# Modulation of two transformer blocks: weights laid out turned, one fused product and sum by VectorE per 128 outputs, no sums by TensorE or GpSimd

## The reference, cut to what matters

```
# first block: dilated and differential attention, then a gated FFN
mod = silu(c) @ w_ada + b_ada                  # 2048 -> 6 x 2048
sh_a, sc_a, gt_a, sh_f, sc_f, gt_f = split(mod, 6)
h = rmsnorm(x, g_pre_attn) * (1 + sc_a) + sh_a
mix = attention(h @ w_in)                      # w_in: 2048 x 6144
x = x + gt_a * rmsnorm(mix @ w_out, g_post_attn)
h = rmsnorm(x, g_pre_ffn) * (1 + sc_f) + sh_f
f = (silu(h @ w_gate) * (h @ w_up)) @ w_down
x = x + gt_f * rmsnorm(f, g_post_ffn)
# second block: mLSTM and a gated convolution side by side
mod = silu(c_2) @ w_ada_2 + b_ada_2            # 2048 -> 3 x 2048
shift, scale, gate = split(mod, 3)
h = rms_norm(x, norm1_w_2) * (1 + scale) + shift
x = x + gate * (merged(h @ w_in_2 + b_in_2) @ w_out_2)
out = rms_norm(x, normf_w_2)
```

## Time and profile before

| | |
|---|---|
| time, median of 3 runs | 2428.45 us (2428.37 to 2431.06) |
| the profiled execution: its own time | 2428.18 us |
| its span | 2426.4 us |
| PE busy | 2335.1 us, 96% |
| DVE busy | 1910.8 us, 79% |
| ACT busy | 1120.4 us, 46% |
| POOL busy | 94.5 us, 4% |
| chain that ended last | PE 84%, DVE 11%, ACT 2% |

### The profile page before, as it was taken

How to read it: one execution, slowest core, us unless ns; L and a number is a source line. 1 busy time by engine, 2 the same in 40 slices (tenths; PEclk the granted TensorE clock), 3 DMA queues, 4 the chain that set the end, 5 groups by cost and what they waited for, 6 DMA issues and landing times.

```text
span 2426.4 us, 26656 instructions
## 1 busy us (share of the span) xinstructions
PE 2335.1 (96%) x10405; PEld 1923.6 (79%) x10405; DVE 1910.8 (79%) x2446; ACT 1120.4 (46%) x1469; POOL 94.5 (4%) x60
## 2 busy tenths in 40 slices
PE   3789999989999999999989999999999999999998
PEld 3578788878888888788868888888888888888887
DVE  7888898977888988999865567898778697555875
ACT  3344566554444444444464333444445544444453
POOL 0000000000110100113100000000000001000000
PEclk8889999999999999999999999999999999999999
DMA  9978788958778778799845655465666557655553
GB/s 348 360 276 303 275 290 330 355 210 282 277 275 295 280 275 292 268 333 354 320 146 199 219 192 201 169 218 192 205 208 206 204 188 269 209 196 195 191 191 122
DMA packets 89694, 601.64 MB, mean 248 GB/s; under 512 B 11072, under 2 KB 11248, under 8 KB 18784
## 3 DMA queue, kind: packets, MB, share of 16 engines
q1 hardware_dynamic: 85520, 588.94, 68.2%
q0 software_dynamic: 3040, 10.37, 1.4%
q10 hardware_dynamic: 1008, 0.62, 0.1%
HBM read 597.75 MB, written 2.14 MB: 247 GB/s over the span
## 4 chain that ended last, share of the span: by engine, by line
PE 84%; DVE 11%; ACT 2%; issue 2%; DMA 1%; DVEq 0%; ACTq 0%
PE PS L1216 19%; PE PS L1217 19%; PE PS L1225 19%; PE PS L1200 16%; PE PS L1205 8%; DVE BIAS L1635 5%; DVE LO L1617 3%; PE PS L1307 1%; DMA RAW<-in_w_down 1%; ACT HI L691 1%; PE PS L1333 0%; DMA R<-in_k_inv 0%; PE PS L1551 0%; DVE R L1665 0%; DMA RAW<-in_w_first 0%
## 5 line engine op out<-in xcount | busy, mean ns | idle before, releaser
L691 ACT ACTIVATE HI<-RAW 128x1024 fp32r<-128x1024 f32 x808 | 854.5, 1061 | 1192.0 <-PE PS L1225 727.1
L1617 DVE TENSOR_TENSOR LO<-RAW,HI 128x1024 fp32r<-128x1024 f32 x808 | 1018.8, 1265 | 422.0 <-ACT HI L691 418.1
L1216 PE MATMUL PS<-HI,XH 128*128 128x512 f32 x2176 | 868.3, 399 | 7.6 <-DVE XL L1871 3.1
L1217 PE MATMUL PS<-HI,XL 128*128 128x512 f32 x2176 | 854.6, 393 | 0.0
L1225 PE MATMUL PS<-LO,XH 128*128 128x512 f32 x2176 | 587.1, 391 | 2.9 <-DVE LO L1617 2.9
L1216 PEld LDWEIGHTS PS<-HI,XH 128*128 128x128 f32 x2176 | 413.0, 190 | 97.1 <-ACT HI L691 4.7
L1225 PEld LDWEIGHTS PS<-LO,XH 128*128 128x128 f32 x2176 | 410.5, 189 | 91.1 <-DVE LO L1617 4.9
L1217 PEld LDWEIGHTS PS<-HI,XL 128*128 128x128 f32 x2176 | 413.1, 190 | 84.4 <-issue 1.0
L1635 DVE SCALAR_TENSOR_TENSOR BIAS<-RAW,CACT,BIAS 128x1024 f32<-128x1024 f32 x270 | 348.8, 1292 | 8.2 <-DMA RAW<-in_w_mod 0.3
L1200 PE MATMUL PS<-HI,XH 128*128 128x512 f32 x1056 | 326.8, 391 | 3.8 <-issue 2.2
L1200 PE MATMUL PS<-HI,XL 128*128 128x512 f32 x1056 | 325.6, 390 | 0.0
(11 more groups left out here) (256 smaller groups left out, 888.6 us busy)
## 6 DMA issues: line engine op xcount, KB each, us to landing
RAW<-in_w_second SPq DMA_DIRECT2D x208, 1024.0 KB, 4.9
RAW<-in_w_mod SPq DMA_DIRECT2D x144, 1024.0 KB, 5.1
RAW<-in_w_ffn SPq DMA_DIRECT2D x88, 1024.0 KB, 4.9
RAW<-in_w_first SPq DMA_DIRECT2D x64, 1024.0 KB, 5.1
RAW<-in_w_down SPq DMA_DIRECT2D x44, 1024.0 KB, 5.0
BIAS<-in_b_in SPq DMA_DIRECT2D x40, 256.0 KB, 5.1
X<-in_x SPq DMA_DIRECT2D x1, 2048.0 KB, 10.8
R<-mod_rows POOLq DMA_DIRECT2D x4, 512.0 KB, 4.9
```

The costliest lines, as they stand in the source:

```text
L691: act.activation(HI[:, (it["half"] + hf) % HLS, :], RAW[:, it["slot"], hf * 1024:(hf + 1) * 1024], ACT.Copy).then_inc(s.hi_ready, 1)
L1216: pe.matmul(PS[:, bank + u, :], XH[:, 2 * n + kk, rows], hi, start=start and kk == 0, stop=False)
L1217: pe.matmul(PS[:, bank + u, :], XL[:, 2 * n + kk, rows], hi, start=False, stop=False)
L1617: dve.tensor_tensor(LO[:, slot, :], RAW[:, it["slot"], hf * 1024:(hf + 1) * 1024], HI[:, slot, :].bitcast(F32), ALU.subtract).then_inc(s.l ...
```

## The change

The weights of the modulation are laid out the other way round: an A now holds 128 outputs on the partitions and all 2048 inputs along the row. Silu(c) is loaded broadcast to all partitions (`C_ROW`, 1 MB, in the place of the accumulators BIAS; `C_ROW_2` for the second block from chunk 96 on), and one DVE instruction (L1543) multiplies a whole A by it and sums along the row into one column of `MOD`. So every A ends with 128 finished outputs. The accumulator chains, the sums by PE, `reduce_ada` and the additions on POOL, MODT and its turn by PE are gone. Shift and scale of the first modulation are laid out in turn, tile by tile, so that four A make one pair of tiles; `first_scale`, `x_pair` and `x_low` go by pairs, at halves 6q and 6q + 4, and the body puts 4 A, 2 A and 2 A ahead of the three W of each q. The number of chunks of either kind stays. Gates go from MOD to DRAM and back as a broadcast row (`gate_rows`).

```diff
 def first_body():
-    body = [("A",)] * 8
-    for q in range(1, 4):
+    body = []
+    for q in range(4):
         for g in range(EARLY):
-            body += [("A",)] * (1, 3, 4)[g] + [("W", EARLY * (q - 1) + g)]
-    for c in range(9, 64):
+            body += [("A",)] * (4, 2, 2)[g] + [("W", EARLY * q + g)]
+    for c in range(12, 64):
...
+            def gate_rows(n, rows):
+
+                v = mod_dram[:, n * D:(n + 1) * D]
+                pool.wait_ge(s.gate_ready, n + 1)
+                pool.dma_start(v[0].rearrange("(t p) -> p t", p=P), MOD[:, GATE_AT[n]:GATE_AT[n] + NK]).then_inc(s.gate_out, 16)
+                pool.wait_ge(s.gate_out, 16 * n + 16)
+                pool.dma_start(rows, v.to_broadcast([P, D])).then_inc(s.gg_in, 16)
...
+            act.dma_start(C_ROW, c_rows[0:1, :].to_broadcast([P, D])).then_inc(s.c_in, 16)
...
-            act.activation(CACT[:].rearrange("p a k -> p (a k)"), CT, ACT.Silu).then_inc(s.cact_ready, 1)
+            act.activation(C_ROW, C_ROW, ACT.Silu).then_inc(s.cact_ready, 1)
...
             def x_pair(n):
 
-                act.wait_ge(s.mod_ready, n // 2 + 1)
+                act.wait_ge(s.mod_ready, n + 1)
...
-                if h < 8 * EARLY and h % (2 * EARLY) < 2:
-                    x_pair(first_half(h)[1])
+                if h < 8 * EARLY and h % (2 * EARLY) in (0, 4):
+                    x_pair(h // EARLY)
...
+                    if h == 20:
+                        act.wait_ge(s.c_2_in, 16)
+                        act.activation(C_ROW_2, C_ROW_2, ACT.Silu).then_inc(s.cact_ready, 1)
...
-            def ada_sum(a, hf):
-                pe.wait_ge(s.ada_step, a * 16 + 16)
-                bank_7_free()
-                used[0] += 1
-                if hf is None:
-                    for t in range(8):
-                        m = pe.matmul(PS[:, 7, t:t + 1], acc_of(a)[:, t * P:(t + 1) * P], ONES[:, 0:1], start=True, stop=True,
-                                      skip_group_check=True)
-                else:
-                    m = pe.matmul(PS[:, 7, :], ONES[:], acc_of(a)[:, hf * 512:(hf + 1) * 512], start=True, stop=True)
-                m.then_inc(s.ada_sum, 1)
...
             def ada_chunk(sec, it):
-                a = sec.ada_group(0, it["ada"])
-                which, acc = vector_of(a), acc_of(a)
+
+                a = sec.ada_chunk(0, it["ada"])
+                w = RAW[:, it["slot"], :]
                 dve.wait_ge(landed[it["slot"]], sec.landed(0, it))
-                for kk in range(2):
-                    k = 2 * it["step"] + kk
-                    w = RAW[:, it["slot"], kk * 1024:(kk + 1) * 1024]
-                    if k == 0:
-                        if 2 <= a <= ADA_BY_PE:
-                            dve.wait_ge(s.ada_sum, SUMS[a - 2])
-                        if a > ADA_BY_PE:
-                            dve.wait_ge(s.acc_reduced, a - ADA_BY_PE)
-                        dve.tensor_scalar(acc, w, CACT[:, which, 0:1], None, ALU.mult).then_inc(s.ada_step, 1)
-                    else:
-                        dve.wait_ge(s.ada_step, a * 16 + k)
-                        dve.scalar_tensor_tensor(out=acc, in0=w, scalar=CACT[:, which, k:k + 1], in1=acc,
-                                                 op0=ALU.mult, op1=ALU.add).then_inc(s.ada_step, 1)
...
+                if a == ADA_OF_C:
+                    dve.wait_ge(s.cact_ready, 2)
+                dve.tensor_tensor_reduce(w, w, C_ROW if a < ADA_OF_C else C_ROW_2, 1.0, 0.0, ALU.mult, ALU.add,
+                                         MOD[:, a:a + 1]).then_inc(s.ada_step, 1)
...
+            def first_scale(n):
+
+                v = MOD[:, 4 * n:4 * n + 4]
+                dve.wait_ge(s.ada_step, 4 * n + 4)
+                link(dve.tensor_tensor(v, v, BCOL[:, 4 * n:4 * n + 4], ALU.add))
+                dve.scalar_tensor_tensor(out=SCALE[:, 2 * n:2 * n + 2], in0=MOD[:, 4 * n + 1:4 * n + 4:2], scalar=1.0,
+                                         in1=COL[:, 2 * n:2 * n + 2], op0=ALU.add, op1=ALU.mult).then_inc(s.mod_ready, 1)
...
                 if it["kind"] == "A":
                     ada_chunk(sec, it)
-                    if it["j"] == 0:
+                    if it["j"] == 1:
+                        first_rstd()
+                    if it["j"] == 2:
                         angles()
                         first_columns()
-                    if it["j"] == 1:
-                        first_rstd()
-                    if it["j"] == 8:
-                        first_scale(0)
+                    if it["ada"] < ADA_FIRST and it["ada"] % 4 == 3:
+                        first_scale(it["ada"] // 4)
```

More of the change, by code:

```diff
@@ L229, in __init__ @@
         self.n_halves = 2 * sum(kind == "W" for kind, *_ in body)
-        self.n_ada = sum(kind == "A" for kind, *_ in body) // 8
+        self.n_ada = sum(kind == "A" for kind, *_ in body)
         assert self.n_chunks % RAWS == 0 and self.n_halves % HLS == 0
@@ L237, in __init__ @@
             slot_gain[slot] += 16
-            self.items.append(dict(kind=kind, what=what, slot=slot, j=j, half=half, ada=ada // 8, step=ada % 8,
+            self.items.append(dict(kind=kind, what=what, slot=slot, j=j, half=half, ada=ada,
                                    landed=slot_gain[slot]))
@@ L409, in build @@
         JUNK = region(6144, 2048)
-        CT = region(16512, 32)
+        C_ROW_2 = region(13312, 2048)
         ANG = region(16640, NT, 96)
@@ new lines, in ada_chunk, with gate @@
+                dve.tensor_tensor_reduce(w, w, C_ROW if a < ADA_OF_C else C_ROW_2, 1.0, 0.0, ALU.mult, ALU.add,
+                                         MOD[:, a:a + 1]).then_inc(s.ada_step, 1)
+                for n, at in enumerate(GATE_AT):
+                    if a == at + NK - 1:
+                        gate(n)
+                if a == MOD_AT[1] + 31:
+                    modulation(2)
+            def gate(n):
+                v = MOD[:, GATE_AT[n]:GATE_AT[n] + NK]
+                dve.wait_ge(s.ada_step, GATE_AT[n] + NK)
+                add = dve.tensor_tensor(v, v, BCOL[:, GATE_AT[n]:GATE_AT[n] + NK], ALU.add)
+                if n == 2:
+                    add.then_inc(s.gate_ready, 1)
+                    return
+                link(add)
+                dve.tensor_tensor(v, v, COL[:, 114 + 16 * n:130 + 16 * n], ALU.mult).then_inc(s.gate_ready, 1)
@@ L2420, in chunks, with in_turn @@
         return np.stack([np.concatenate(p, axis=2).reshape(P, 2048) for p in pieces])
[L2422 to L2429 removed]
+    turned = [w[name].T.reshape(-1, P, D) for name in ("w_ada", "w_ada_2")]
+    def in_turn(a, b):
+        return np.concatenate([np.stack([a[0:NK], a[NK:2 * NK]], axis=1).reshape(-1, *a.shape[1:]), a[2 * NK:], b])
     def first():
@@ L2450, in columns @@
         return np.concatenate([np.asarray(v).reshape(-1, P).T for v in vectors], axis=1)
-    b_ada = np.asarray(inputs["b_ada"])[0]
-    return {"w_mod": chunks(modulation()), "w_first": chunks(first()), "w_ffn": chunks(ffn()),
+    b_ada, b_ada_2 = (np.asarray(inputs[name])[0].reshape(-1, P) for name in ("b_ada", "b_ada_2"))
+    return {"w_mod": in_turn(*turned), "w_first": chunks(first()), "w_ffn": chunks(ffn()),
             "w_down": w["w_down"].reshape(NKF, P, 2048), "w_second": chunks(second()),
```

237 lines of the change are left out of this document (62 added, 175 removed).

## The result

The changed kernel takes 2434.86 us (median of 11 runs, 2433.88 to 2436.99), the kernel before 2430.84 (median of 11 runs beside it). Two runs of the kernel before, of 2629.38 and 5899.89 us, lie far above the others and are left out of the comparison; without them its median is 2428.91. The ratio of the other runs is 1.0022, 95% interval 1.0013 to 1.0032: the changed kernel is slower by some 5 us, hardly more than a measurement tells from no change. The profiled execution took 2434.49 us, with a span of 2432.7, 6.3 more than in the earlier trace rows.

The account below looks back on a forecast made before the run. PE bounds the kernel (busy 2335.1 of 2426.4 us), paced by DVE in the first 160 us. From 2428.18: + 23.4 start and groups, - 14.3 PE's sums, - 3.0 DVE's relief, - 4.4 POOL, giving 2429.9 us, range 2415 to 2445.

Parts of the forecast that it names:

- The start and the groups: First 160 us: half 1 at 55.3, then 37.3 us per group in place of 31.76 as DVE stands waiting.
- The load of C_ROW ahead of IDENT: Start, ACT's queue: the 1 MB ahead of IDENT adds up to 2.6 us, so the turn starts at 26.1.
- Halves 19 to 23: End of the early part: five halves take 13.6 + 2.8 = 16.4 us, 2.8 being the low clock's price.
- the loss at half 24: End of the early groups: half 24 starts at 183.6 in place of 160.21, a loss of 23.4 us.
- the third rival: Early groups longer than 37.3 us, DVE waiting for an A's load; decides from 1 us per group (2433.4); chance 0.27.
- The half pace: Rival on the new DVE product: an A takes 4.4 us, the kernel 2545 us; chance 0.03.
- The sums and the relief: Behind the start: PE's dropped sums gain 14.3 us (10.5 to 17), DVE's cheaper A 3.0 (0 to 10).
- POOL: Reductions that stretch DVE's LO halves, and the gate's additions, end: a gain of 4.4 us (bounds 3 and 5).
- costed at nothing: Gates' way through DRAM: no cost, covered over 100 us ahead of use; without cover, 0 to some 10 us.
- The most likely case: Whole kernel: losses and gains cancel, 2423.6 to 2433.3 us, within 0.2%; chance 0.44.

Follow-up runs that it names:

- e1: Changed kernel with the old order of the early chunks, both pairs of a group modulated ahead of its first half: 2413.48 us, ratio 0.9936.
- e4: Changed kernel with eight A first, then three W in each early group, both pairs modulated ahead of the first half: 2412.90 us, ratio 0.9937.
- e7: Kernel of e2 with one extra DVE instruction of 0.42 us behind each of the first 32 A: 2442.07 us.
- e11: Changed kernel with IDENT loaded ahead of C_ROW on ACT's queue: 2432.39 us.
- e5: Kernel of e2 with PE's sums put back as products nobody reads: 2443.00 us.
- e6: Kernel of e2 with six of GpSimd's eight partition reductions put back, on numbers nobody reads: 2432.28 us, ratio 1.0008.
- e9: Kernel of e6 with one extra DVE instruction of 0.42 us behind each A from chunk 80 on: 2437.90 us, ratio 1.0029.
- e10: Kernel of e2 with one extra DVE instruction of 0.42 us behind each A from chunk 80 on, without the reductions: 2431.38 us, ratio 1.0003.
- e3: Changed kernel with the edits of e1 and e2 together: 2406.95 us, ratio 0.991.
- e2: Changed kernel with the gate turned on DVE and stored in 64 pieces of 128 bytes, not 2048 of 4 bytes: 2431.61 us, ratio 1.0008.

## Why the prediction held, step by step

**The start and the groups** were right in mechanism. Half 0 was put at 38.2 and came at 39.20, half 1 at 55.3 and 55.58. The group was put at 37.3 and was 36.4, 36.5 and 35.4; the A in it cost 2.21 and not 2.3, since the read of the sum hides, which is 0.7 us per group, and the rest was not traced. Halves 19 to 23: 16.4 predicted, 16.43 measured. So the loss at half 24 was 20.1 where the sum had 23.4. That the order makes most of it is shown by e1 and e4 (half 24 comes 22.6 us earlier), that each us of a group counts over three times by e7. The load of C_ROW ahead of IDENT, which the prediction put at 2.6 us for IDENT, costs 3.3 at half 24 (e11). The mechanism of the third rival, DVE waiting for the load of an A, did not occur: from 40 to 157 us DVE waits for ACT alone.

**The half pace** of the fused product with two operands in SBUF did not occur: 2.285 us for 2048 columns are 896 columns per us, against 1024 / 1.22 = 839 in the earlier trace rows, the row with one tensor read twice. The Trainium skill (page "Vector Engine (DVE) Microarchitecture Reference", section "Points that are easy to get wrong") says that instructions of the form S2S2D2_STT halve their throughput with two sources in SBUF that are not bf16, by which the prediction estimated 4.4. The trace disagrees with that for this instruction, which it calls CUSTOM_DVE_ANT_0; whether the page means it, no run can tell.

**The sums and the relief** were put at 14.3 and 3.0 and came to 17.7 together; e5 gives the sums 13.5 by places and 11.4 by medians. The bounds of the sums were added up wrongly: with all column sums at 3.4 they make 17.5 and not 17, with all at 1.94 11.7 and not 10.5. The forecast doesn't hang on that.

**POOL** was put at 4.4 and the stretch of trace shows 4.9, but the reason given, the stretched LO halves, does not carry it, and that this number came out is luck. The earlier trace rows was misread: its last row holds three reductions (at 996.83, 1066.76 and 1133.41) and not six, the rest of POOL's 37.35 us being mostly the gate's additions, and the row of 174.08 us, which served as the measure without them, holds two. e6 shows that reductions alone cost little, e9 and e10 that they cost more with a dearer A; what the 4.9 us were made of is open in part.

**The step that failed** is the one "costed at nothing": "gate 0 is whole more than 100 us ahead of its use". The cover looked at was for who needs the gate, and there it held. What was missed is whom the transfer disturbs: for 13.2 us the store took the DMA engines from the weight chunks, and PE lost 7.4 us at a place that has nothing to do with the gate. Gates 1 and 2 have the same store at 724 and 2026 us; from 732 to 736 the core moved 59 GB/s, and from 2030 to 2034 33, but PE was busy throughout.

**The clock** in the passage to the second block was not in the sum: the same 202 products take 53.46 us in place of 52.25, at a mean granted clock of 0.87 in place of 0.90. PE is busy for 45.43 us in place of 43.95, so it is the products that take longer and not the waits. The row of the kernel before:

```profile
1246.03:1298.28 52.25, 43.95 (x202) 34.30 (x201) 36.15 (x49) 33.88 (x58) 1.63 (x3) 0.90 0.44 152
```

Why the clock was lower stays open.

The outcome lies 5 us above the number: 2429.9 against 2434.86, or 4.6 above it in the profiled execution: + 7.4 for the store and + 1.4 in the FFN and the passage not foreseen, - 3.3 at the start, - 0.4 in the sums and the relief, - 0.5 for POOL. That the number is so near is partly luck, as errors of either sign stand against each other. The most likely case, a time within 0.2%, was narrowly missed; the time is 0.22% longer, but not for the reason that stood there, longer groups.

## What to carry to other kernels

When one instruction replaces many, ask what order it was written in for: here the product, with the sums it makes needless, was worth 22 us in the old order (e3), and the new order of the first chunks and an 8 KB store gave all of it back. A transfer is hidden only if it is also harmless to the stream beside it: in this kernel the number of its pieces decided that, not its bytes (e2). And a price that two causes make together (e6, e9, e10) can't be read from the one that is seen in the timeline: look for the same event in a stretch that lost nothing, as the LO half at 807.94.

## What the runs showed of the hardware

A store of 8 KB in 2048 pieces of four bytes took 13.2 us and in the windows of 4 us meanwhile the core moved 254, 70 and 119 GB/s, then 330 and 428; in four stores of together 64 pieces of 128 bytes it landed in 4.5 us (median) and the windows from 330 to 346 show 336 to 428 GB/s. The fused product and sum takes 2.285 us for 128x2048 with two different float32 operands in SBUF, the same pace as with one tensor read twice (1.22 us for 128x1024). A partition reduction of GpSimd stretched a DVE instruction beside it from 1.22 to 5.56 us in e6 as in the kernel before, and one of 128x16 from 0.18 to 4.40 us.
